# One transformer layer in float32 on one core: the gate products' weight sums, ring and order changed

## The reference

```python
proj = h @ w_in[l]
(aq, ak, av, ag, bq, bk, bv, bf, bg, cq, cg, mg) = split_columns(proj)
...
for n in range(N_BRANCH):
    gate = jax.nn.sigmoid(mg[..., n * D_MODEL:(n + 1) * D_MODEL] + b_gate[l, n])
    term = gate * (branches[n] @ w_branch[l, n])
    merged = term if merged is None else merged + term
y = merged @ w_out[l]
```

## Time and profile before

| | |
|---|---|
| Median of three runs | 1909.7 us (1909.49 to 1909.95) |
| The profiled execution's own time | 1909.92 us |
| Its span, first to last instruction | 1908.4 us |
| PE busy | 1878.7 us (98%) |
| DVE busy | 1171.8 us (61%) |
| ACT busy | 790.1 us (41%) |
| POOL busy | 127.4 us (7%) |
| Gate stage, in the span | 986.5 to about 1446.4 us |

### The profile page before, as it was taken

How to read it: one execution, slowest core, us unless ns; L and a number is a source line. 1 busy time by engine, 2 the same in 40 slices (tenths; PEclk the granted TensorE clock), 3 DMA queues, 4 the chain that set the end, 5 groups by cost and what they waited for, 6 DMA issues and landing times.

```text
span 1908.4 us, 25193 instructions
## 1 busy us (share of the span) xinstructions
PE 1878.7 (98%) x9079; PEld 1568.5 (82%) x9079; DVE 1171.8 (61%) x1852; ACT 790.1 (41%) x1319; POOL 127.4 (7%) x187
## 2 busy tenths in 40 slices
PE   8999999999999999999989999999999999999997
PEld 6888887888888888888878888888888888888987
DVE  5743334655455545777778878878887544567436
ACT  4652222544444444344445555555455333342111
POOL 1100000100000000000000000000001000000004
PEclk9999999999999999999999999999999999999999
DMA  8843333333333333333251451533629444454322
GB/s 301 280 136 100 109 99 88 99 101 82 98 101 90 90 92 92 98 104 93 78 212 44 178 178 54 210 105 116 221 72 326 148 155 144 147 212 143 134 89 89
DMA packets 223005, 253.14 MB, mean 133 GB/s; under 512 B 12192, under 2 KB 158160, under 8 KB 220880
## 3 DMA queue, kind: packets, MB, share of 16 engines
q1 hardware_dynamic: 202848, 189.82, 31.5%
q0 software_dynamic: 20080, 62.30, 9.7%
HBM read 218.89 MB, written 31.03 MB: 131 GB/s over the span
## 4 chain that ended last, share of the span: by engine, by line
PE 97%; POOL 1%; DVE 0%; ACT 0%; DMA 0%; issue 0%; POOLq 0%; SPq 0%; ACTq 0%; DVEq 0%
PE acc L554 13%; PE acc L556 13%; PE acc L555 13%; PE scores L876 4%; PE scores L878 4%; PE scores L874 4%; PE acc L874 3%; PE acc L876 3%; PE acc L878 3%; PE transposed L581 3%; PE scores L944 2%; PE scores L945 2%; PE scores L946 2%; PE acc L944 2%; PE acc L945 2%; PE acc L946 2%
## 5 line engine op out<-in xcount | busy, mean ns | idle before, releaser
L1401 DVE TENSOR_TENSOR w_lo<-raw_weights,w_hi 128x1024 fp32r<-128x1024 f32 x246 | 300.1, 1223 | 370.0 <-ACT w_hi L1021 364.8
L1021 ACT ACTIVATE w_hi<-raw_weights 128x1024 fp32r<-128x1024 f32 x246 | 259.8, 1059 | 401.6 <-PE acc L556 115.6
L554 PE MATMUL acc<-h_hi,w_lo 128*128 128x512 f32 x1056 | 420.7, 398 | 0.0
L556 PE MATMUL acc<-h_hi,w_hi 128*128 128x512 f32 x1056 | 412.0, 390 | 0.0
L555 PE MATMUL acc<-h_lo,w_hi 128*128 128x512 f32 x1056 | 411.1, 389 | 0.0
L1271 ACT ACTIVATE piece_split<-w 128x512 fp32r<-128x512 f32 x336 | 212.2, 632 | 221.3 <-PE acc L878 81.2
L1833 DVE TENSOR_TENSOR piece_split<-w,piece_split 128x512 fp32r<-128x512 f32 x336 | 232.0, 691 | 87.4 <-ACT piece_split L1271 78.5
L556 PEld LDWEIGHTS acc<-h_hi,w_hi 128*128 128x128 f32 x1056 | 198.2, 188 | 42.4
L554 PEld LDWEIGHTS acc<-h_hi,w_lo 128*128 128x128 f32 x1056 | 198.9, 188 | 41.0 <-issue 2.8
L555 PEld LDWEIGHTS acc<-h_lo,w_hi 128*128 128x128 f32 x1056 | 198.6, 188 | 39.7 <-issue 1.0
L874 PE MATMUL scores<-piece_split,h_sums 128*128 128x512 f32 x216 | 84.0, 389 | 0.0
(11 more groups left out here) (374 smaller groups left out, 3516.9 us busy)
## 6 DMA issues: line engine op xcount, KB each, us to landing
raw_weights<-in_w_in SPq DMA_DIRECT2D x134, 512.0 KB, 3.8
w<-in_w_in SPq DMA_DIRECT2D x96, 512.0 KB, 8.6
raw_weights<-in_w_branch SPq DMA_DIRECT2D x48, 512.0 KB, 5.3
raw_weights<-in_w_mem_kv SPq DMA_DIRECT2D x32, 512.0 KB, 6.2
raw_weights<-in_w_out SPq DMA_DIRECT2D x32, 512.0 KB, 3.8
gate<-gate_scratch POOLq DMA_DIRECT2D x12, 1024.0 KB, 6.6
gate_scratch<-first_product POOLq DMA_DIRECT2D x12, 512.0 KB, 6.7
x_buf<-in_x SPq DMA_DIRECT2D x4, 1024.0 KB, 8.6
```

The source lines that it names most:

```text
L554: pe.matmul(bank_out, wl, hi[:, k, :], start=first, stop=False)
L556: return pe.matmul(bank_out, wh, hi[:, k, :], start=False, stop=last)
L1021: act.activation(w_hi[:, slot, :], raw[:, slot, :], ACT.Copy).then_inc(hi_ready, 1)
L1401: dve.tensor_tensor(w_lo[:, slot, :], raw[:, slot, :], w_hi[:, slot, :].bitcast(F32), ALU.subtract).then_inc(lo_ready, 1)
```

## The change

**Sums by DMA.** DVE's `weight_sum` is gone. Three slots x, y, z stay: x holds block 11, y block 22, z block 21. POOL issues DMAs that add to what a slot holds (`accum_op=ALU.add`): to x block 12 from DRAM after G1's pieces and block 22 after G5's, to y block 12 after G3's, and to z the slot x itself after G6's. Each adds four pieces, 1024 KB, and there are eight in a group. ACT waits for them in `piece_hi`. The slots' sums now differ in sign from before, so `h_sums` and two of the copies negate. SP issues 12 loads of 512 KB in a group instead of 16.

**Ring of eight.** `p_split` has eight slots. Four of them lie where `w_21` was, in space that branch A uses until it is gated, so that ACT waits for `gated` before piece 2 of the first group.

**Tile by tile.** PE now runs the eight pieces of a product for tile 0, then again for tile 1. A slot is freed in the second pass only. A copy of tile 0 is made in front of the next product's piece 0, a copy of tile 1 in front of its piece 7.

**Order.** The products run G1, G2, G5, G3, G6, G7, G4 (before: G1, G5, G6, G2, G7, G3, G4).

```diff
-G1, G5, G6, G2, G7, G3, G4 = range(PRODUCTS)
+G1, G2, G5, G3, G6, G7, G4 = range(PRODUCTS)
 PIECES = PRODUCTS * BT
+PRING = 8
...
             def gate_product(g, p, banks, first, stop, freed=None):
+
                 hi, lo = left[p]
-                for k in range(BT):
-                    n = piece(g, p, k)
-                    pe.wait_ge(pc_lo, n + 1)
-                    wh, wl = (p_split[:, n % RING, v, :] for v in range(2))
-                    for t in range(2):
-                        tok = slice(t * P, (t + 1) * P)
+                for t in range(2):
+                    tok = slice(t * P, (t + 1) * P)
+                    if freed is not None:
+                        pe.wait_ge(freed, 2 * g + t + 1)
+                    for k in range(BT):
+                        n = piece(g, p, k)
+                        if t == 0:
+                            pe.wait_ge(pc_lo, n + 1)
+                        wh, wl = split_piece(n, 0), split_piece(n, 1)
...
+                        if t == 1:
+                            last.then_inc(pc_mult, 1)
+                        elif k == BT - 1:
+                            last.then_inc(pc_first, 1)
...
             def piece_hi(g, p, k):
                 n = piece(g, p, k)
                 if p in loaded:
                     act.wait_ge(pc_loaded[loaded[p]][k // 4], 32 * (g + 1))
                 else:
-                    act.wait_ge(t_ready, t_index(g, summed[p], k) + 1)
-                if n >= RING:
-                    act.wait_ge(pc_mult, n - RING + 1)
+                    act.wait_ge(t_summed[summed[p]][k // 4], (16 if p in (G5, G6) else 32) * (g + 1))
+                if n >= PRING:
+                    act.wait_ge(pc_mult, n - PRING + 1)
...
+            def copy_after(g, p, t):
+
+                z, y, x = gate_banks(g)
+                if p == G1:
+                    if g:
+                        act.wait_ge(st_c21, 16 * g)
+                    copy_out(g, p, t, z[t], s1_buf, ev_s1)
...
+            act.wait_ge(gated, 3 * BT)
             for g in range(GROUPS):
-                z, y, x = gate_banks(g)
                 for p in range(PRODUCTS):
                     for k in range(BT):
+                        if k == 0 and (g or p):
+                            copy_after(g if p else g - 1, p - 1 if p else G4, 0)
+                        if k == BT - 1 and (g or p):
+                            copy_after(g if p else g - 1, p - 1 if p else G4, 1)
                         if g or p or k >= 2:
                             piece_hi(g, p, k)
...
-                        if g == GROUPS - 1 and p in (G3, G4) and k % 2:
+                        if g == GROUPS - 1 and p in (G7, G4) and k % 2:
                             branch_hi(2, k // 2 + (4 if p == G4 else 0))
...
+            def sum_weights(g, t, dst, src, p, d):
+
+                pool.wait_ge(pc_lo, piece(g, p, 4 * d + 3) + 1)
+                pool.dma_start(dst[:, 4 * d:4 * d + 4, :], src, accum_op=ALU.add).then_inc(t_summed[t][d], 16)
+
             for g in range(GROUPS):
+                for d in range(2):
+                    sum_weights(g, "1", w_x, gate_weights(g, 0, 1, 4 * d, 4), G1, d)
+                if g:
+                    pool.wait_ge(ev_c21, 2 * g + 2)
+                    store_gate(g - 1, 0, 1, s1_buf, st_c21)
+                for d in range(2):
+                    sum_weights(g, "2", w_x, gate_weights(g, 1, 1, 4 * d, 4), G5, d)
+                pool.wait_ge(ev_c11, 2 * g + 2)
+                store_gate(g, 0, 0, s1_buf, st_c11)
+                for d in range(2):
+                    sum_weights(g, "3", w_y, gate_weights(g, 0, 1, 4 * d, 4), G3, d)
+                for d in range(2):
+                    pool.wait_ge(pc_lo, piece(g, G2, 4 * d + 3) + 1)
+                    sum_weights(g, "4", w_z, w_x[:, 4 * d:4 * d + 4, :], G6, d)
                 if g == GROUPS - 1:
                     pool.wait_ge(pc_mult, piece(g, G6, BT))
                     load_branch(2, brc_raw[:, :, :])
+                pool.wait_ge(ev_c12, 2 * g + 4)
+                store_gate(g, 1, 0, u2_buf, st_c12)
...
```

More of the change, by code:

```diff
@@ L279, in program, with gate_weights, split_piece @@
     b2_row = at(R2 + 14336, "ln_b_row", [P, D], F32)
+    def gate_weights(g, half_k, half_n, k, count):
+        n, b = N_BRANCH - 1 - g // 2, g % 2
+        col = MG + n * D + b * BW + half_n * 512
+        row = half_k * BW + k * P
+        return w_in[0][row:row + count * P, col:col + 512].rearrange("(k p) n -> p k n", p=P)
+    def split_piece(n, v):
+        slot = n % PRING
+        return p_split[slot // (PRING // 2)][:, slot % (PRING // 2), v, :]
     with ExitStack() as ctx:
@@ L379, in program @@
         s3_split = sem("s3_split")
-        pc_loaded = {w: [sem(f"pieces_{w}_{d}_loaded") for d in range(2)] for w in ("11", "12", "22", "21")}
+        pc_loaded = {w: [sem(f"pieces_{w}_{d}_loaded") for d in range(2)] for w in "xyz"}
+        t_summed = {t: [sem(f"weight_sum_{t}_{d}") for d in range(2)] for t in "12"}
+        for t in "34":
+            t_summed[t] = [sem(f"weight_sum_{t}")] * 2
         pc_hi = sem("pieces_hi_ready")
@@ L509, in _ @@
                         sp.wait_ge(pc_lo, piece(g - 1, G7, 2 * d + 1) + 1)
-                    load_pieces(g, "12", w_12, 0, 1, d)
-                for d in range(4):
-                    if g:
-                        sp.wait_ge(pc_lo, piece(g - 1, G3, 2 * d + 1) + 1)
-                    load_pieces(g, "22", w_22, 1, 1, d)
-                if g == 0:
-                    sp.wait_ge(gated, 3 * BT)
+                    load_pieces(g, "y", w_y, 1, 1, d)
                 for d in range(4):
@@ L1275, in gate_banks, with copy_out, copy_c21 @@
                 return (a, b, c) if g % 2 == 0 else (c, b, a)
-            def copy_out(banks, dst, done):
-                for t in range(2):
-                    act.activation(dst[:, t, :], banks[t][:, :], ACT.Copy).then_inc(done, 1)
-            def copy_c21(g):
-                act.wait_ge(pc_mult, piece(g + 1, G1, 0))
+            def copy_out(g, p, t, bank_in, dst, done):
+                if t == 0:
+                    act.wait_ge(pc_first, PRODUCTS * g + p + 1)
+                else:
+                    act.wait_ge(pc_mult, piece(g, p, BT))
+                act.activation(dst[:, t, :], bank_in[:, :], ACT.Copy).then_inc(done, 1)
+            def copy_c21(g, t):
                 act.wait_ge(st_c11, 16 * (g + 1))
-                copy_out(gate_banks(g)[0], s1_buf, ev_c21)
+                copy_out(g, G4, t, gate_banks(g)[0][t], s1_buf, ev_c21)
             def branch_hi(n, k):
@@ L1330, in _ @@
                 split_hi_now(CH_M + n)
-            copy_c21(GROUPS - 1)
+            for t in range(2):
+                copy_c21(GROUPS - 1, t)
             def merged_hi(k):
@@ L1729, in h_sums @@
                 steps.settle()
-                steps.mark(dve.tensor_tensor(part(S1, 1), part(S1, 0), part(S1, 1), ALU.add))
+                steps.mark(dve.tensor_tensor(part(S1, 1), part(S1, 1), part(S1, 0), ALU.subtract))
                 dve.tensor_tensor(s3_buf[:, :].unsqueeze(1), part(S2, 0), part(S1, 0), ALU.subtract)\
@@ L1856, in gate_banks, with add_out, add_after @@
                 return (a, b, c) if g % 2 == 0 else (c, b, a)
-            def add_out(banks, buf, done):
-                for t in range(2):
-                    dve.tensor_tensor(buf[:, t, :], banks[t][:, :], buf[:, t, :], ALU.add).then_inc(done, 1)
+            def add_out(g, p, t, bank_in, buf, copied_to, negate, done):
+                if t == 0:
+                    dve.wait_ge(pc_first, PRODUCTS * g + p + 1)
+                else:
+                    dve.wait_ge(pc_mult, piece(g, p, BT))
+                dve.wait_ge(copied_to, 2 * g + t + 1)
+                if negate:
+                    dve.scalar_tensor_tensor(out=buf[:, t, :], in0=bank_in[:, :], scalar=-1.0, in1=buf[:, t, :],
+                                             op0=ALU.mult, op1=ALU.subtract).then_inc(done, 1)
+                else:
+                    dve.tensor_tensor(buf[:, t, :], bank_in[:, :], buf[:, t, :], ALU.add).then_inc(done, 1)
+            def add_after(g, p, t):
+                z, y, x = gate_banks(g)
+                if p == G2:
+                    add_out(g, p, t, x[t], s1_buf, ev_s1, False, ev_c11)
+                if p == G7:
+                    add_out(g, p, t, z[t], s5_buf, ev_s5, True, ev_c22)
             def branch_lo(n, k):
@@ L1894, in _ @@
+                        if g == 0 and p == G3 and k == 4:
                             dve.wait_ge(s3_hi, 1)
                             dve.tensor_tensor(h_lo[:, 0:BT, HALF:SEQ], h_lo_raw[:, 0:BT, HALF:SEQ],
[L1896 to L1900 removed]
@@ L1910, in _ @@
+                                .then_inc(s3_split, 1)
+                        if g == GROUPS - 1 and p in (G7, G4) and k % 2:
                             branch_lo(2, k // 2 + (4 if p == G4 else 0))
+            dve.wait_ge(pc_lo, PIECES * GROUPS)
             for n in range(LOOKAHEAD):
```

154 lines of the change are left out of this document (49 added, 105 removed).

## The result

The changed kernel takes 1973.1 us in the median of four runs (1970.12 to 1975.03), the kernel before 1909.8 us. The ratio is 1.033 (95% interval 1.0312 to 1.0348): 63.3 us slower, with 1978 us forecast and 1930 to 2010 as the range.

The account below looks back on a forecast made before the run. The prediction took PE, busy 1878.7 of 1908.4 us, to bound the kernel. Its terms, 1.4 + 45 + 22 = 68 us on the profiled 1909.92, gave 1978.3, forecast as 1978 us; range 1930 to 2010, its own 1965 to 1993.

Parts of the forecast that it names:

- What bounds the kernel: In the gates PE is busy throughout each 76.6 us group except 2.1 us in the first, all the gates can return.
- DVE's relief at 0: Removing DVE's 32 sums per group, about 0.6 us each, gains 0 because PE is full beside it.
- The tile passes and the ring at 0: Pieces are ready before PE's next product needs them: 0 us; tightest at G7, ready T0 + 2.2, needed T0 + 2.7.
- The start: First product: PE has only one pass of two pieces to do before piece 2 is ready, +1.4 us.
- The store of block 21: Groups 1 to 5: store lands behind two adds, T0 (group start) + 15.0 to 16.8, delaying G2; +45 us.
- The 2 us for the clock: Added to each 7 us wait at G2 in groups 1 to 5, for matmuls at the lower clock behind it.
- The double price of an add: An adding DMA costs twice a load, 5.6 to 6.4 us per 1024 KB, since two operands must pass.
- the cheap rival: An add costs as a load: store lands at T0 + 10.5, five waits of 1.5 us, 1936 us; chance 22%.
- Branch C: Group 5: ACT waits for branch C's load after G7's piece 1, other G7 pieces queued behind; +22 us.
- The term L: Landing of branch C's load, counted from G7's start T0: T0 + 10 to 21, 16 taken.
- The one wait of some 20 us that I named as a sign: In group 5 PE waits some 20 us for a piece of G7, ACT ahead of it waiting for branch C.
- The sums at 0: The adds end before G4's second half of weights is needed at T0(G6) + 23.2, costing 0 at double price.

Follow-up runs that it names:

- Experiment 8: The kernel before with DVE's 32 weight sums of each group left out, semaphores kept, so the sums are not formed: 1909.2 us, ratio 0.9997.
- experiment 7: Changed kernel with block 21's store issued before the adds, ACT's branch A wait at piece 4, branch C's eight splits behind G4's last piece: 1913.2 us.
- experiment 9: On experiment 7, PE multiplies pieces 0 and 1 for both tiles first in the first group's first product: 1910.2 us, ratio 1.0001.
- experiment 10: Changed kernel with one edit: PE multiplies pieces 0 and 1 for both tiles first in the first group's first product: 1969.1 us, ratio 1.0308.
- experiment 4: Changed kernel with the eight adding DMAs of a group turned into plain copies, so the weight sums are not formed: 1935.5 us, ratio 1.0135.
- experiment 1: Changed kernel with POOL issuing block 21's store ahead of the next group's first two adding DMAs: 1930.8 us, ratio 1.0113.
- experiment 2: Changed kernel with branch C's eight splits on ACT and DVE moved behind pieces 4 to 7 of G4, two behind each: 1958.5 us, ratio 1.0252.
- experiment 3: Changed kernel with the edits of experiment 1 and experiment 2 together: 1918.7 us, ratio 1.0049.
- experiment 5: Changed kernel with ACT's two copies of G1 moved behind G2's eight pieces, POOL's queue order kept: 1931.3 us, ratio 1.011.
- experiment 6: On experiment 3, ACT waits for branch A's release before piece 4 of the first group, not piece 2: 1917.2 us, ratio 1.004.

## Why the prediction was right, step by step

- **What bounds the kernel, and DVE's relief at 0.** Right. Experiment 8 took the relief alone and found 0.6 us.
- **The tile passes and the ring at 0.** Right. In experiment 7 PE has no wait from the one in the first product to the end of the gates, G7 with its half microsecond to spare included.
- **The start, forecast 1.4 us, measured 4.0.** The mechanism was right: the missing 1.4 us of work stands behind the wait. The term was mis-sized in its last step. I let a wait of 2.1 us keep the clock (as the row before showed) and did not ask what the longer wait would do. It was 2.83 us, and a slow stretch of some 6 us at half pace followed, which cost 2.9 us. The 1.1 us that are left stand against the forecast 1.4. Experiments 9 and 10 show that both go when PE takes both tiles first.
- **The store of block 21, forecast 45 us, measured 40.2.** The chain held at each link: the issue at T0 + 3.2 (forecast 3.1), the adds' landings at T0 + 7.9 and T0 + 13.7 (8.0 to 8.8 and 13.6 to 15.2), the store at T0 + 15.0 (15.0 to 16.8), 2.0 us from there to PE. The waits average 5.9 us (forecast 7, the low end 6.0) and the slow stretch costs 2.1 us each (forecast 2). What was off was the price per 1024 KB: between the two landings lie 5.8 us, the rate of all 16 engines doubled (5.6), not that of a lone queue doubled (6.4). My middle value lay between the two. The 2 us for the clock came out near, but the row they were read from did not show them: it is the program's start, where PE had run nothing but eight transposes ahead of the wait. That a stream at full pace falls to half after such a wait is first shown by groups 1 to 5.
- **The double price of an add.** Right. The copies of experiment 4 landed in 5.8 us against 8.6 and 11.3, and they left 1.0 us of wait where the cheap rival had 1.5. That rival was about right for another kernel: 1936 us forecast, 1935.5 measured when the adds are copies. That it fits to half a microsecond is in part luck, since its start was 2 us too low and its wait too high. The range from 1930 to 2010 holds this rival too, so the total alone does not tell the two apart; the landings do. The Trainium skill's page "Collectives: The Full Stack", section "The bandwidth ceiling: the fold count and why AG ≠ RS ≠ AR", says of ReduceScatter, whose add needs two source reads, that it runs at half of AllGather's rate. The page measured transfers between cores; the adding DMA here agrees, with 5.8 us per 1024 KB against the 2.8 us of plain transfers, and 203 GB/s against 377.
- **Branch C, forecast 22 us, measured 18.1.** The mechanism was right, queue position and all. The term L was mis-sized: T0 + 11.2, not 16. I had the adds ahead end at T0 + 4.5 to 9.5 and SP's weights compete; the last of them was issued at 1460.49 and landed after 12.2 us, at T0 + 3.5, and the load took 10.7 us, 0.9 more than before. Nor did the double price matter here: with copies in place of the adds the load took 11.1 us and the place cost 17.7. From L the step to the end of the pass was 12.1 us (forecast 10.1), since the matmuls behind the wait ran at half pace. The one wait of some 20 us that I named as a sign came as two, 11.7 and 1.9 us.
- **The sums at 0.** Right. No wait for a sum reached PE in any run.

The errors of two terms (5 and 4 us too much) and of the third (2.6 too little) leave the sum 6 us and the forecast 5 us too high. The third error hid a part of the other two.

## What to carry to other kernels

Where one engine is full, as PE was here, moving work off another gained nothing; read what the moved work is now in front of, in each in-order queue, and what waits behind it. Here a late landing cost only through what was queued behind the instruction that waited for it, so either end of the chain could be mended: the issue order on one engine or the copy's place on another gave back the same 42 us. In this kernel a DMA that adds cost what twice its bytes cost in a plain load, and a PE wait of 5.4 to 6.6 us cost about two more for the slow stretch behind it.

## What the runs showed of the hardware

- A DMA that adds to SBUF used the DMA engines about twice as long as a plain load: from 1073 to 1081, with such DMAs in flight and none of SP's, the 16 engines were busy throughout and moved 203 GB/s, against 377 GB/s before. A window that moves 203 GB/s need not have free engines; the DMA share tells.
- A DMA that adds to SBUF from DRAM has a row of 1.3 us on POOL at its issue, against 0.77 for the copy of the same shape in experiment 4 and 0.88 for an add from SBUF. Two in a row took 2.69 us (experiment 1). The next row can start before the add's ends: the store of block 21 starts 0.78 us after the add, and its own row is then 1.26 us long in place of 0.72.
- The clock at the start went with PE's order. With 12 matmuls of the gates ahead of the wait (the kernel before, experiments 8, 9 and 10; waits of 2.09, 1.2, 1.2 and 1.6 us) it stayed at its upper level. With 6 (the changed kernel and experiments 1 to 7; waits of 2.15 to 2.84 us) it was at the lower level behind the wait: in experiments 4 and 5 it had not risen before, in the six others it fell, in three of them while PE waited and in experiments 1, 2 and 7 0.3 to 0.6 us after PE had resumed. The runs do not separate the length of the wait from the work ahead of it.
- A slow stretch behind a wait of 5.4 to 6.6 us cost 1.6 to 2.6 us.
